# A low-part subtract for the second feed-forward's entry, on GpSimd in place of VectorE

## The reference, cut to what matters

```python
y = merged @ w_out[l]
x = x + ga1 * rmsnorm(y, g_post_mix[l])

h = rmsnorm(x, g_pre_ffn[l]) * (1.0 + sc2) + sh2
u = jax.nn.relu(h @ w_ff1[l])
y = (u * u) @ w_ff2[l]
x = x + ga2 * rmsnorm(y, g_post_ffn[l])
```

## Time and profile before

| | |
|---|---|
| median of 3 runs | 768.65 us (767.84 to 768.71) |
| profiled execution | 767.42 us, its span 765.4 us |
| PE busy | 96% of the span |
| DVE busy | 550.0 us, 72% |
| ACT busy | 384.1 us, 50% |
| GpSimd busy | 51.3 us, 7% |
| mean granted TensorE clock | 0.994 of full speed |

### The profile page before, as it was taken

How to read it: one execution, slowest core, us unless ns; L and a number is a source line. 1 busy time by engine, 2 the same in 40 slices (tenths; PEclk the granted TensorE clock), 3 DMA queues, 4 the chain that set the end, 5 groups by cost and what they waited for, 6 DMA issues and landing times.

```text
span 765.4 us, 13235 instructions
## 1 busy us (share of the span) xinstructions
PE 735.9 (96%) x5336; PEld 677.8 (89%) x5336; DVE 550.0 (72%) x940; ACT 384.1 (50%) x546; POOL 51.3 (7%) x72
## 2 busy tenths in 40 slices
PE   5999998999999999998999999999998999999996
PEld 4999986789999999987999999999877999998995
DVE  6797788676787776866669977885986777555554
ACT  7433767655443334446444446565554444444442
POOL 2940000000000000000432000000000000000000
PEclk9999999999999999999999999999999999999999
DMA  8636411357888888661454556544542675545611
GB/s 330 222 119 230 157 60 53 123 208 301 325 340 319 310 323 322 222 221 55 144 191 134 185 221 217 194 173 166 173 176 91 244 260 211 199 165 185 219 56 55
DMA packets 27022, 151.10 MB, mean 197 GB/s; under 512 B 3128, under 2 KB 7836, under 8 KB 9564
## 3 DMA queue, kind: packets, MB, share of 16 engines
q1 hardware_dynamic: 22620, 124.81, 45.2%
q10 hardware_dynamic: 3456, 25.17, 8.2%
q0 software_dynamic: 896, 0.43, 0.3%
HBM read 148.92 MB, written 1.05 MB: 196 GB/s over the span
## 4 chain that ended last, share of the span: by engine, by line
PE 77%; DVE 15%; ACT 4%; issue 2%; DMA 1%; SPq 0%; DVEq 0%; ACTq 0%
PE ps L460 23%; PE ps L461 23%; PE ps L462 23%; DVE ada L1718 3%; DVE w_lo L1628 2%; DMA raw<-wts 1%; PE ps L590 1%; ACT w_hi L1191 1%; PE ps L566 1%; PE ps L1010 1%; DVE extra L1881 1%; DVE rows_ga L1764 1%; ACT rows_ga L1266 0%; PE ps L957 0%; PE ps L533 0%
## 5 line engine op out<-in xcount | busy, mean ns | idle before, releaser
L1628 DVE TENSOR_TENSOR w_lo<-raw,w_hi 128x2048 fp32r<-128x2048 f32 x106 | 239.8, 2269 | 109.2 <-ACT w_hi L1191 109.0
L460 PE MATMUL ps<-h_hi,w_hi 128*128 128x256 f32 (+2 forms) x1000 | 285.7, 286 | 2.3 <-ACT alibi L1451 1.3
L462 PE MATMUL ps<-h_hi,w_lo 128*128 128x256 f32 (+2 forms) x1000 | 282.8, 283 | 0.0
L461 PE MATMUL ps<-h_lo,w_hi 128*128 128x256 f32 (+2 forms) x1000 | 282.8, 283 | 0.0
L1191 ACT CAST w_hi<-raw 128x2048 fp32r<-128x2048 f32 x106 | 198.6, 1886 | 48.7 <-PE ps L462 38.1
L460 PEld LDWEIGHTS ps<-h_hi,w_hi 128*128 128x128 f32 (+2 forms) x1000 | 190.2, 190 | 6.1 <-issue 4.9
L461 PEld LDWEIGHTS ps<-h_lo,w_hi 128*128 128x128 f32 (+2 forms) x1000 | 190.2, 190 | 1.8 <-issue 0.7
L462 PEld LDWEIGHTS ps<-h_hi,w_lo 128*128 128x128 f32 (+2 forms) x1000 | 190.2, 190 | 0.2
L460 PE MATMUL ps<-w_hi,mix_hi 128*128 128x512 f32 x248 | 97.8, 394 | 1.0 <-DVE small L1764 0.8
L461 PE MATMUL ps<-w_lo,mix_hi 128*128 128x512 f32 x248 | 96.8, 390 | 0.0
L462 PE MATMUL ps<-w_hi,mix_lo 128*128 128x512 f32 x248 | 96.5, 389 | 0.0
(11 more groups left out here) (309 smaller groups left out, 963.9 us busy)
## 6 DMA issues: line engine op xcount, KB each, us to landing
raw<-wts SPq DMA_DIRECT2D x113, 1024.0 KB, 4.8
ada<-w_ada ACTq DMA_DIRECT2D x24, 1024.0 KB, 5.1
resid<-x SPq DMA_DIRECT2D x2, 512.0 KB, 4.1
raw<-wts SPq DMA_DIRECT2D x2, 512.0 KB, 6.5
rows_ga<-rows_wide SPq DMA_DIRECT2D x1, 1024.0 KB, 7.0
out<-resid SPq DMA_DIRECT2D x4, 256.0 KB, 2.0
shared<-shared SPq DMA_DIRECT2D x2, 320.0 KB, 6.8
raw<-w_idx SPq DMA_DIRECT2D x1, 544.0 KB, 4.0
```

The lines of the kernel that those rows point to most:

```text
L460: nc.tensor.matmul(o, lh, rh, start=start, stop=False)
L461: nc.tensor.matmul(o, lh, rl, start=False, stop=False)
L462: return nc.tensor.matmul(o, ll, rh, start=False, stop=stop)
L1628: V.tensor_tensor(w_lo[:, s % RING, 0:w], raw[:, n_of[name] % RAW, 0:w], w_hi[:, s % RING, 0:w].bitcast(F32), ALU.subtract).then_inc(w_rea ...
```

## The change

DVE no longer makes the low part of `fa1`. GpSimd does, in one instruction at the end of its list, after it has waited for ACT's high part. It signals on a semaphore of its own, `fa1_ready`, since `x_ready` is counted by DVE. PE waits for the new semaphore ahead of the products with `fa1`. SP waits, ahead of the loop of loads, for `x_ready` at `fa0`'s number and for the new semaphore.

```diff
--- before.py
+++ after.py
@@ -281,6 +281,7 @@
         b_z, b_zm, b_abs, b_ln, b_sp, b_c, b_cm, b_att = (sem(n) for n in (
             "b_scores_ps", "b_masked", "b_abs", "b_ln", "b_softplus", "b_sum_ps", "b_sum_masked", "b_att"))
         up_ps, up_a, m_sum, m_hi, m_lo = (sem(n) for n in ("up_ps", "up_used", "merged", "merged_hi", "merged_lo"))
+        fa1_ready = sem("fa1_ready")
         fa_tile, fa_turned, fa_first_hi, fa_first = sem("fa_tile"), sem("fa_turned"), sem("fa_first_hi"), sem("fa_first_ready")
         sqy, y_gain, y_res = sem("squares"), sem("y_gained"), sem("y_residual")
 
@@ -383,7 +384,8 @@
                         load_loop(FF1_LOOP, TURNS_1)
                 elif kind == "s" and s_idx[name] in ff2_tiles:
                     if s_idx[name] == FF2_LOOP:
-                        sp.wait_ge(x_ready, x_no["fa1"])
+                        sp.wait_ge(x_ready, x_no["fa0"])
+                        sp.wait_ge(fa1_ready, 1)
                         load_loop(FF2_LOOP, TURNS)
                 else:
                     load(name)
@@ -452,6 +454,10 @@
                 for b in (0, HD):
                     for to, at in ((b, b + 8), (b + 8, b)):
                         pool.dma_start(partner(r)[to:to + 8, :], src[at:at + 8, :]).then_inc(s_swap[r], 16)
+
+            hi, lo = extras["fa1"]
+            pool.wait_ge(x_hi, x_no["fa1"])
+            nc.gpsimd.tensor_tensor(lo, raw_of("fa1"), hi.bitcast(F32), ALU.subtract).then_inc(fa1_ready, 1)
 
         @block.tensor
         def _(pe):
@@ -1104,7 +1110,7 @@
                 fa = [[a.rearrange("p (k c) -> p k c", k=DC) for a in extras[f"fa{st}"]] for st in range(2)]
                 pe.wait_ge(x_ready, x_no["fa0"])
                 rows_tile(*fa[0], fa_bank(0), 0, rows(0))
-                pe.wait_ge(x_ready, x_no["fa1"])
+                pe.wait_ge(fa1_ready, 1)
                 rows_tile(*fa[1], fa_bank(1), 0, done)
                 keep_warm(6, 4)
                 turn_rows2(1)
@@ -2238,7 +2244,6 @@
             modulated("g_pre_ffn", 32)
             dve.wait_ge(x_new, 10)
             post_rows(0)
-            extra_low("fa1")
             split_rows2(0)
             post_rows(1)
             split_rows2(1)
```

## The result

| | before | after |
|---|---|---|
| median, us | 768.69 (767.84 to 769.17, 5 runs) | 772.67 (771.85 to 773.02, 5 runs) |
| profiled span, us | 765.4 | 769.9 |
| DVE busy, us | 550.0 | 552.2 |
| GpSimd busy, us | 51.3 | 56.1 |
| mean granted clock | 0.994 | 0.991 |

The change makes the kernel slower: ratio 1.0051, 95% interval 1.0036 to 1.0065, so 2.8 to 5.0 us. The forecast was 772.6.

A forecast was written before the change was run, and what follows sets the result against it. PE bounds the kernel nearly everywhere, but DVE bounds the entry from 562 to 579 us. Hold +4.1, relief -0.5 and clock +0.4 gave +4.0 us, so 772.6 us on the median, range 769.7 to 774.8.

The forecast's parts named there:

- Hold: DVE's row chain from about 563.7 us: stands still while GpSimd's estimated 4.8 us subtract reads SBUF, +4.1 us.
- fixed part of 0.51 us after the hold: End of a GpSimd instruction, after it lets go of the common way to SBUF: 0.51 us, read from early scaling.
- Mechanism: DVE instructions with two SBUF inputs and GpSimd instructions reading SBUF exclude each other for whole instructions; chance 0.79.
- no block: Rival for DVE's row chain: both engines read freely, DVE loses nothing, end 0.5 us earlier at 768.1; chance 0.07.
- Short turns: Rival for DVE's row chain: GpSimd reads in small batches with DVE in between, about +0.7 us, 769.3; chance 0.11.
- slow GpSimd: Rival for GpSimd's subtract: twice as slow, holding DVE 8.6 us, +8.5 us in all, 777.1; chance 0.03.
- Relief: DVE's h splits for the first 128 tokens: without the 2.29 us subtract they end 0.5 us earlier.
- Clock: PE's first row transposes: after a longer idle gap, part runs at 1.2 GHz, +0.4 us.
- slack: PE ahead of the second rows' transposes: its 0.67 us wait absorbs what PE loses on the first tile's slices.
- Bounds: Limits on DVE's standstill: lower 1.6 us for one pass and 3.2 for two operands, upper 8.6 us.
- Sum: Whole kernel: +4.1 - 0.5 + 0.4 = +4.0 us, giving 772.6 us on the median.
- If GpSimd began some us later, the block would fall on the h splits and cost the same: DVE's h splits after normalisation: a later GpSimd start costs the same +4 us, as they are critical too.

The follow-up runs named there:

- e4_late: The change with GpSimd's full subtract started only after the first rows are normalised; ratio 1.0031 against the kernel before, stretch +2.85 us.
- e8_pieces: The change with GpSimd's subtract cut into eight instructions of 256 columns, PE waiting piece by piece; ratio 1.0041 against the kernel before.
- e6_copy: The change with GpSimd copying the raw tile, one operand, in place of the subtract (low part wrong); ratio 1.0006 against the kernel before.
- e1_half: The change with GpSimd subtracting only columns 1024 to 2047 and DVE the first 1024; ratio 1.0025 against the kernel before.
- e3_write: The change with GpSimd filling the low part with zeros, reading nothing, in place of the subtract; ratio 1.0001 against the kernel before.
- e0_sem: The kernel before with only the new semaphore and changed waits, DVE keeping its subtract; ratio 1.0000 against the kernel before.
- e7_split: The kernel before, no GpSimd subtract: DVE makes 1280 columns in its first wait for ACT, 768 in its second; ratio 0.9996 against it.
- e5_warm: The change with 18 filler matmuls in PE's idle time ahead of the first rows' transposes; ratio 1.0046 against the kernel before.

## Why the prediction was right

- *Hold.* Forecast 4.1 us, measured 4.24. The length was estimated at 4.8 us; it is 4.52 where nothing stands in its way (e4_late), and 4.77 in the change, where it started beside DVE's residual add. The Trainium skill (GPSIMD Engine Reference, "Elementwise — side-by-side cycle accounting") has 4497 ns for a tensor_tensor add of 2048 float32 columns; the 4.52 us of e4_late's subtract agree. That the scaling from a 256-column, one-input instruction came so near was luck: a subtract of 256 columns takes 0.73 us (e8_pieces), less than the 0.87 of that one-input instruction, and a copy of 2048 columns 2.13 us (e6_copy), so GpSimd's price per column depends on the operation. And the fixed part of 0.51 us after the hold, read from the early rows, was near 0.15 here. In e8_pieces a 256-column subtract costs DVE 0.41 to 0.56 us, twice or more the 0.20 of the 256-column scaling in the earlier trace rows.
- *Mechanism.* Exclusion by whole instructions stands against each rival that was run: size (e1_half), writing (e3_write), waits (e0_sem), place (e4_late), pieces (e8_pieces). The rival "no block" is out by the 4.93 us square sum. "Short turns" inside one instruction is out too: one DVE instruction bore all of the hold. (Its sum had a slip: the rows show eight short DVE instructions up to 566.6, not about a dozen. Its 0.8 to 1.6 us fit eight; less the relief that is +0.3 to +1.1.) The slow GpSimd is out by 4.77 us. That the same rule covers a one-input cast of DVE is shown by e4_late.
- *Relief.* Forecast 0.5, measured 0.52 to 0.53 (e3_write, e7_split).
- *Clock.* Forecast +0.4, measured 0.38 and, taken away, 0.39 (e5_warm). PE stood 0.38 us ahead of the second transposes in place of 0.67, so the slack took the rest, as forecast.
- *Bounds.* The hold lay well between them. The lowest, 1.6 us for one pass over 2048 columns, is what a one-operand copy came to (1.58, e6_copy).
- *Sum.* +4.0 forecast, +4.11 in the traces, +3.98 in the medians.
- *One step was wrong.* "If GpSimd began some us later, the block would fall on the h splits and cost the same" does not hold: e4_late costs 2.85 us. I had left out that DVE waits for ACT from the normalised rows to the first split, and GpSimd's first 1.4 us go there. It had no part in the sum.

## What to carry to other kernels

Work moved from VectorE to GpSimd is not off VectorE's path when it reads SBUF: in these runs VectorE's instructions with two SBUF inputs, even one-column ones, and its wide casts and scalings stood still almost until GpSimd's instruction ended, and 2.3 us taken away cost 4.2. Ask of such a move what VectorE executes beside it, and put it where VectorE waits anyway, or give GpSimd work that only writes (a fill held nothing in e3_write). Before that, look whether the piece can be cut to fit VectorE's own waits.

## What was not expected

**A DVE instruction with one SBUF input was held too.** The cast of 256 columns in e4_late, 3.23 us in place of 0.29, and in e8_pieces the normalisation with its scalar from SBUF, 1.18 in place of 0.75. The Trainium skill (SBUF — State Buffer, "Who interferes with whom") says that copy, cast and tensor_scalar can run in a mode that takes both of VectorE's ways to SBUF, and can then contend with GpSimd; these two rows agree. Their pace fits as well: 1024 columns take 0.75 us in the normalisation and 1.22 in a two-input subtract (e1_half), 256 columns 0.29 us in the cast and 0.42 in the subtract behind it.

**The clock fell after shorter gaps, too.** In e6_copy PE had been idle for 2.19 us ahead of the transposes, and they took 1.60 in place of 1.10 us; the granted clock from 570 to 574 was 0.58:

```profile
570.25 1.60 PE L1076 MATMUL ps<-consts,z 128*128 128x128 f32 x8 [2.19 <-DVE z L2231]
```

In e1_half it was 2.57 us of idle time and 1.85 us of transposes.

**The executions differ ahead of the edit.** The residual add starts anywhere from 562.29 (before) to 564.46 (e0_sem), though the programs do the same work up to there. PE's granted clock between 50 and 100 us differs as well: 0.97 in the profiled execution of before, 0.93 in that of e0_sem:

```profile
50.00:100.00 50.00, 49.08 (x411) 46.85 (x410) 39.72 (x120) 28.46 (x56) 0.00 (x0) 0.93 0.48 170
```

The two go together only in part. The three executions with 0.93 start the add at 564.28 to 564.46, the four with 0.97 at 562.29 to 562.63; but the three with 1.00 there (e8_pieces, e1_half, e5_warm) start it at 562.77, 563.55 and 564.06. The cause stays open. A difference of half a microsecond is therefore to be read from a stretch of the trace and not from the times.

What makes GpSimd's subtract last more than twice as long as its copy of the same 2048 columns (4.52 and 2.13 us) is open as well.
